# Second conv block read and multiplied ahead of the fifth modulation block, in a one-core diffusion layer on Trainium2

## The chip, the cores and the metric

The kernel runs on one core of one Trainium2 chip. The metric is the device time of one execution in microseconds (us). All times below are in us unless marked ns. PE is the matmul engine, PEld its weight load, DVE the vector engine, ACT the scalar engine, POOL the GpSimd engine, SP the engine whose queue issues nearly all loads.

## The reference

A layer with parallel token mixers and a mixture of experts, for 128 context tokens (s = 0) and 128 latent tokens (s = 1), 1024 channels, batch 1. The part around the change is the adaLN modulation and the combined input projection:

```python
mod = silu(c) @ w_ada + b_ada                 # 1024 x 6144; c_ctx for the context tokens
shift1, scale1, gate1, shift2, scale2, gate2 = split(mod, 6)
h = rmsnorm(x, norm1_g) * (1 + scale1) + shift1
z = h @ w_in                                  # 1024 x 8192
q, v, zf, zb, og, u, gz = split(z, ...)       # u: 2 x 512 columns of the conv branch
u = u[:, :512] * sigmoid(u[:, 512:])          # then a width-31 depthwise convolution
...                                           # gated linear recurrence with q, v, zf, zb
x1 = x + gate1 * (merged branches @ w_out)
x2 = x1 + gate2 * moe(rmsnorm(x1, norm2_g) * (1 + scale2) + shift2)
```

## The kernel before

Weights come in blocks of 1024 x 512 numbers (2048 KB each). `w_ada` has twelve of them and `w_in` sixteen. The list `blocks` fixes the order of the loads, and the sync engine's stream issues them in that order, one DMA each, from one line (L543). A block lies in one of four buffers, `ring[0]` to `ring[3]`, which the instruction listings below call ring_49 to ring_52. The table `place` says which. `load_block` waits until the block that had this buffer before is done with (`released`), and only then issues; everything behind it in the SP stream waits with it. Three rules of release matter here:

```python
if name in split[:apart]:
    eng.wait_ge(w_lo_done, 4 * split.index(name) + 4)
elif name[:3] == "ada":
    eng.wait_ge(part_ready, ADA.index(int(name[3:])) + 1)
elif name == "u1":
    eng.wait_ge(u1_part_ready, 1)
```

A modulation block (`ada...`) is used by `ada_partial(j)` (L1656 in `ada_partial`): eight matmuls of a padded 32-column condition vector with the block, 128x512 each, 16 in the records since each float32 matmul is recorded twice. The number j counts the blocks in the order 2, 3, 0, 1, 4, 5, ..., 11 (`ADA`), so j = 4 to 11 are the blocks ada4 to ada11. They accumulate in one bank, and the first of them, j = 4, opens it. Their sums (gates, second shift and scale) are first read behind the first quarter of block v0 (`ada_sums(2)`).

The projection blocks u2, q0, zf0, zb0, q1, zf1 and zb1 are multiplied in split precision: ACT rounds a quarter of the block to `w_hi` (L768), DVE computes the remainder `w_lo` (L1076), and PE runs three groups of eight matmuls per quarter, `h_hi` by `w_hi`, `h_hi` by `w_lo`, `h_lo` by `w_hi` (L1709, L1711, L1714 in `project_parts`). Such a block is released once DVE has split its last quarter. The modulated input is split too: `h_hi` on ACT (L783) and `h_lo` on DVE (L1100). ACT makes four of the eight channel blocks of `h_hi`, then the first quarter of `w_hi` of u2, then the other four, in this order of its program. The first conv block u1 is multiplied unsplit (L1695) with the modulation blocks j = 2 and 3 in the midst of it, followed by eight matmuls for its shift (L1787).

PE's program then runs ada_partial(4) and, for each of the seven names, its four quarters followed by one further modulation block, j = 5 to 11. Behind that come v0, v1 and the other projections (L1753, L1709 and so on), the recurrence (L1769, L1771), the merge and the experts (L2117, L2173), whose weights come in chunks of 1024 KB.

Of the kernel before, what the change touches and what calls it, by code (L numbers as in the profile page):

```python
# [132 lines left out]
def build(nc, A, outs):  # L133
    y_prompt, y_sample, new_state = outs
    ctx = ExitStack()
    with ctx:
# [186 lines left out]
        def cols(w, c0):  # L323
            return w.rearrange("(k p) c -> p k c", p=P)[:, :, c0:c0 + 512]
# [4 lines left out]

        ADA_GROUPS = ((0, 2), (2, 2), (4, 8))  # L330
        ada_group_of = [g for g, (_, n) in enumerate(ADA_GROUPS) for _ in range(n)]
        ada_sums_at = [256 + 8 * ADA[first] for first, _ in ADA_GROUPS]
        ada_after = {name: 4 + n for n, name in enumerate(("u1", "u2", "q0", "zf0", "zb0", "q1", "zf1", "zb1"))}
        col_of = {"u1": U0, "u2": U0 + 512, "v0": V0, "v1": V0 + 512}
        for half in range(2):
            for name, c0 in (("q", Q0), ("zf", ZF0), ("zb", ZB0), ("og", OG0), ("ga", GZ0), ("gb", GZ0 + 1024)):
                col_of[f"{name}{half}"] = c0 + 512 * half
        blocks = []
        for name in ("ada2", "ada3", "u1", "ada0", "ada1", "ada4", "u2", "q0", "ada5", "zf0", "ada6", "zb0", "ada7", "q1", "ada8", "zf1", "ada9", "zb1",
                     "ada10", "v0", "ada11", "v1", "og0", "og1", "ga0", "ga1", "gb0", "gb1"):  # L340
            blocks.append((name, cols(w_ada, 512 * int(name[3:])) if name[:3] == "ada" else cols(w_in, col_of[name])))
        blocks.append(("pc", A["w_proj_conv"][0].rearrange("(k p) c -> p k c", p=P)))
# [4 lines left out]
        apart = len(split)  # L347
        split += ["v0", "v1", "og0", "og1", "ga0", "ga1", "gb0", "gb1", "ph0", "ph1", "wo0", "wo1"]
        number = {name: n for n, (name, _) in enumerate(blocks)}


        place = {name: n % 4 for name, n in number.items()}
        for name, n in zip(("u2", "q0", "ada5", "zf0", "ada6", "zb0", "ada7", "q1", "ada8", "zf1", "ada9", "zb1", "ada10", "ada11"),
                           (3, 0, 2, 1, 3, 0, 2, 1, 3, 0, 2, 1, 3, 3)):
            place[name] = n
        for n, name in enumerate(("v0", "v1", "og0", "og1", "ga0", "ga1", "gb0", "gb1", "pc", "ph0", "ph1", "wo0")):
            place[name] = n % 3
# [22 lines left out]
        def tile_of(name):  # L380

            src = blocks[number[name]][1]
            k, n = src.shape[1], src.shape[2]
            return ring[place[name]][:, 0:k * n].rearrange("p (k c) -> p k c", k=k)
# [29 lines left out]
        for name, n, by in ([(f"xt{j}", 1, "act") for j in range(4)] + [(f"h{j}", 1, ("dve", "act")[j % 2]) for j in range(4)]  # L414
# [5 lines left out]
            for j in range(n):  # L420
# [3 lines left out]
                else:  # L424
                    n_dve += 1
                    fills.append((name, j, dve_evac, n_dve))
        fill_no = {(name, j): n for n, (name, j, _, _) in enumerate(fills)}

        def fill_bank(name, j=0):
# [107 lines left out]
        def _(sp):  # L537
            def load_block(name):

                before = in_place[place[name]].index(name) - 1  # L540
                if before >= 0:
                    released(sp, in_place[place[name]][before])
                sp.dma_start(tile_of(name), dict(blocks)[name]).then_inc(s_w[place[name]], 16)  # L543
# [5 lines left out]
                sp.dma_start(x_tok[:, s, :], x[0]).then_inc(s_x, 16)  # L549
            for name, _ in blocks[1:-2]:  # L550
                load_block(name)
                if name == "u2":
                    sp.dma_start(consts[:, C_MASK:C_TRI], A["consts"][:, C_MASK:C_TRI]).then_inc(s_wr, 16)
                    sp.dma_start(b_router[:, :], A["router_bias"].broadcast_to([P, NE])).then_inc(s_wr, 16)
            filled(sp, "gb1", 1)
# [72 lines left out]
            for step in range(FIXED_STEPS, NSTEPS):  # L628
# [10 lines left out]
                for part in range(3):  # L639
                    for item in range(ITEMS_OF[step]):  # L640
                        if part == 0:
                            j = FIRST_ITEM[step] + item
# [16 lines left out]
            n = sp.value_load(nwork, min_val=0, max_val=NX)  # L659
# [958 lines left out]
        def _(pe):  # L1618
            mm = nc.tensor.matmul

            def arrived(name):
                loaded(pe, name)
# [22 lines left out]
            def ada_partial(j):  # L1645

                g = ada_group_of[j]
                first, n = ADA_GROUPS[g]
                arrived(f"ada{ADA[j]}")
                if g == 2 and j == first:  # L1650
                    pe.wait_ge(part_copied, 1)
                w = tile_of(f"ada{ADA[j]}")
                window = slice(14 - 2 * (j - first), 46 - 2 * (j - first))
                for k in range(KD):
                    q = k % 4
                    ins = mm(bank[4 + g % 2][32 * q:32 * q + 32, :], c_pad[:, k, window], w[:, k, :], start=(j == first and k < 4), stop=(j == first + n - 1 and k >= 4))  # L1656
                ins.then_inc(part_ready, 1)
# [41 lines left out]
            def project_parts(name, q):  # L1699


                n = split.index(name)
                b = open_fill(name, q // 2) if q % 2 == 0 else fill_bank(name, q // 2)
                out = b[:, (q % 2) * T:(q % 2 + 1) * T]
                pe.wait_ge(w_lo_done, 4 * n + q + 1)
                for k in range(KD):
                    if (n, q) == (0, 0):
                        pe.wait_ge(h1_hi_done, k + 1)
                    mm(out, part_hi(n, q)[:, k, :], h1_hi[:, k, :], start=(k == 0), stop=False)  # L1709
                for k in range(KD):  # L1710
                    mm(out, part_lo(n, q)[:, k, :], h1_hi[:, k, :], start=False, stop=False)  # L1711
                pe.wait_ge(h1_lo_done, KD)
                for k in range(KD):
                    ins = mm(out, part_hi(n, q)[:, k, :], h1_lo[:, k, :], start=False, stop=(k == KD - 1))  # L1714
                ins.then_inc(proj_ready if q % 2 else w_used, 1)
# [70 lines left out]
                g = k % 4  # L1786
                ins = mm(bank[6][32 * g:32 * g + 32, :], shift_pad[:, k, :], tile_of("u1")[:, k, :], start=(k < 4), stop=(k >= 4))  # L1787
            ins.then_inc(u1_part_ready, 1)
            ada_partial(4)

            for name in ("u2", "q0", "zf0", "zb0", "q1", "zf1", "zb1"):

                for q in range(4):
                    project_parts(name, q)
                if name == "u2":
                    pe.wait_ge(u1_part_ready, 2)
                    for c in range(4):
                        ins = mm(bank[6][:, 2 * c:2 * c + 2], u1_part[:, c * P:(c + 1) * P], consts[:, C_SUM:C_SUM + NS], start=True, stop=True)
                    ins.then_inc(u1_bias_ready, 1)
                ada_partial(ada_after[name])  # L1800

            for level, name in zip(range(-1, LEVELS), ("v0", "v1", "og0", "og1", "ga0", "ga1", "gb0", "gb1")):
                quarter(name, 0)
# [529 lines left out]
```

## Time and profile before

| what | value |
| --- | --- |
| device time, median of 3 runs | 857.24 us (856.8 to 858.62) |
| the profiled execution: its own time | 856.77 us |
| the profiled execution: span | 854.9 us |
| PE busy | 801.4 us (94%) |
| PEld, DVE, ACT, POOL busy | 546.8, 384.8, 234.1, 20.9 us |
| DMA | 284.72 MB, 333 GB/s mean |
| chain that ended last, by engine | PE 68%, SP queue 17%, DMA 10%, DVE 3%, issue 2% |

The span is the time from the first to the last recorded instruction. The profiled execution's own time is 1.87 us longer than its span. The chain that ended last is followed back from the last instruction, at each step to what released it; a stretch of PE in it is a stretch in which any idle time of PE would lengthen the whole.

### The profile page before, as it was taken

The page shows a single profiled execution, that of the slowest core. Times are in us where ns is not written, and L with a number is a line of the kernel's source. Part 1 is how long each engine was busy: PE and PEld are TensorE (multiplying, and loading weights), DVE is VectorE, ACT ScalarE, POOL GpSimd, SP SyncE. Part 2 cuts the span into 40 slices and gives each one's busy share as a digit, 9 for nine tenths or more (in the row PEclk, how much of TensorE's full clock was granted, in tenths as well). Part 3 has the DMA queues.
Part 4 walks back from the last instruction along what each step waited for, and adds up shares of the span by engine and source line. Part 5 has one row for each costly group of instructions (what it writes and reads, how often), then busy time and mean ns, then how long its engine had stood idle before and what let it go on. Part 6 is the DMA issues. An engine that isn't in the chain of part 4 may idle for free.

```text
span 854.9 us, 12931 instructions
## 1 busy us (share of the span) xinstructions
PE 801.4 (94%) x5258; PEld 546.8 (64%) x5258; DVE 384.8 (45%) x789; ACT 234.1 (27%) x388; POOL 20.9 (2%) x22
## 2 busy tenths in 40 slices
PE   3989999999999989989999999599999999799974
PEld 1769898999999989955446355254554835355212
DVE  1157999879987566583323322112221112122114
ACT  2163747344354243231111111011121101011002
POOL 1000010100000000100000000000000000000000
PEclk9999999999999999999999999899999999899988
DMA  8998989323524649889999999999999999999995
GB/s 322 387 387 317 316 280 330 114 100 108 190 99 156 207 149 363 327 307 401 363 416 417 415 418 419 416 416 420 414 417 410 417 415 418 416 418 418 416 413 196
DMA packets 81222, 284.72 MB, mean 333 GB/s; under 512 B 5256, under 2 KB 12040, under 8 KB 64520
## 3 DMA queue, kind: packets, MB, share of 16 engines
q1 hardware_dynamic: 80664, 282.55, 85.0%
q10 hardware_dynamic: 496, 1.30, 0.4%
q8 instruction: 44, 0.72, 0.3%
q14 instruction: 18, 0.15, 0.0%
HBM read 280.67 MB, written 3.16 MB: 332 GB/s over the span
## 4 chain that ended last, share of the span: by engine, by line
PE 68%; SPq 17%; DMA 10%; DVE 3%; issue 2%; ACT 0%; POOL 0%; DVEq 0%; POOLq 0%
SPq L625 15%; PE bank L2117 12%; PE bank L2173 6%; PE bank L1709 6%; PE bank L1711 6%; PE bank L1714 6%; DMA chunk<-in_w_expert_gate_up 5%; PE bank L1695 3%; PE bank L2024 3%; PE bank L2001 3%; PE bank L1771 3%; PE bank L1753 3%; DMA chunk<-in_w_expert_down 3%; PE bank L1656 2%; PE bank L1731 2%
## 5 line engine op out<-in xcount | busy, mean ns | idle before, releaser
L2117 PE MATMUL bank<-chunk,xg 128*64 128x512 f32 (+2 forms) x1024 | 202.8, 627 | 19.0 <-DMA chunk<-in_w_expert_gate_up 18.8
L2117 PEld LDWEIGHTS bank<-chunk,xg 128*64 128x64 f32 (+2 forms) x1024 | 62.7, 131 | 152.4 <-issue 137.1
L2173 PE MATMUL bank<-chunk,act_t 128*64 128x512 f32 (+2 forms) x480 | 97.4, 613 | 1.8 <-DMA chunk<-in_w_expert_down 1.7
L1508 DVE SCALAR_TENSOR_TENSOR act_r<-bank,w_slot,sil 128x256 f32<-128x256 f32 x26 | 12.6, 484 | 182.2 <-ACT sil L981 182.2
L1520 DVE TENSOR_TENSOR y_lo<-bank,y_hi 128x512 fp32r<-128x512 f32 x52 | 35.9, 691 | 73.2 <-ACT y_hi L994 73.2
L981 ACT ACTIVATE sil<-bank 128x256 f32<-128x256 f32 x26 | 10.0, 384 | 210.9 <-PE bank L2117 210.9
L1076 DVE TENSOR_TENSOR ring_lo<-ring,ring_hi 128x1024 fp32r<-128x1024 f32 x44 | 52.7, 1219 | 19.9 <-ACT ring_hi L768 19.7
L2173 PEld LDWEIGHTS bank<-chunk,act_t 128*64 128x64 f32 (+2 forms) x480 | 30.0, 130 | 48.4 <-issue 47.5
L994 ACT ACTIVATE y_hi<-bank 128x512 fp32r<-128x512 f32 x52 | 30.9, 597 | 101.5 <-PE bank L2173 97.7
L1136 DVE SCALAR_TENSOR_TENSOR conv<-upad,dw,conv 128x256 f32<-128x256 f32 x120 | 52.8, 512 | 0.0
L768 ACT ACTIVATE ring_hi<-ring 128x1024 fp32r<-128x1024 f32 x44 | 44.4, 1052 | 25.6 <-PE bank L1735 14.1
L2001 PE MATMUL bank<-sel_p,h_hi 128*128 128x256 f32 x192 | 48.5, 294 | 0.0
L2001 PE MATMUL bank<-sel_p,h_lo 128*128 128x256 f32 x192 | 46.8, 282 | 0.0
L2024 PE MATMUL bank<-y_hi,sel_t 128*128 128x512 f32 x104 | 44.8, 431 | 1.4 <-DVE y_lo L1520 1.4
L1437 DVE COPY xg<-bank 128x512 f32<-128x512 f32 x26 | 17.9, 690 | 54.4 <-PE bank L2001 54.4
L2024 PE MATMUL bank<-y_lo,sel_t 128*128 128x512 f32 x104 | 40.9, 394 | 0.0
L1076 DVE TENSOR_TENSOR w_lo<-ring,w_hi 128x1024 fp32r<-128x1024 f32 x28 | 33.1, 1219 | 12.7 <-ACT w_hi L768 12.7
L2001 PEld LDWEIGHTS bank<-sel_p,h_hi 128*128 128x128 f32 x192 | 36.5, 190 | 0.5
L2001 PEld LDWEIGHTS bank<-sel_p,h_lo 128*128 128x128 f32 x192 | 36.6, 191 | 0.0
L2024 PEld LDWEIGHTS bank<-y_hi,sel_t 128*128 128x128 f32 x104 | 19.5, 187 | 24.3 <-issue 18.5
L1709 PE MATMUL bank<-h_hi,w_hi 128*128 128x256 f32 x224 | 32.4, 287 | 2.6 <-issue 2.6
L1709 PEld LDWEIGHTS bank<-h_hi,w_hi 128*128 128x128 f32 x224 | 28.8, 191 | 8.8 <-issue 6.0
(319 smaller groups left out, 1212.3 us busy)
## 6 DMA issues: line engine op xcount, KB each, us to landing
chunk<-in_w_expert_gate_up SPq DMA_DIRECT2D x128, 1024.0 KB, 21.1
chunk<-in_w_expert_down SPq DMA_DIRECT2D x63, 1024.0 KB, 22.5
ring<-in_w_in SPq DMA_DIRECT2D x16, 2048.0 KB, 10.2
ring<-in_w_ada SPq DMA_DIRECT2D x12, 2048.0 KB, 14.5
ring<-in_w_proj_hgrn SPq DMA_DIRECT2D x2, 2048.0 KB, 7.9
ring<-in_w_out SPq DMA_DIRECT2D x2, 2048.0 KB, 13.8
ring<-in_w_proj_conv SPq DMA_DIRECT2D x1, 2048.0 KB, 7.8
chunk<-in_w_shared_gate_up SPq DMA_DIRECT2D x2, 1024.0 KB, 22.9
```

The source lines that it names most:

```text
L625: sp.dma_start(dst, src).then_inc(s_chunk[place], 16)
L768: nc.scalar.activation(part_hi(n, q), tile_of(split[n])[:, :, q * P:(q + 1) * P], ACT.Copy).then_inc(w_hi_done, 1)
L1076: V.tensor_tensor(part_lo(n, q), tile_of(split[n])[:, :, q * P:(q + 1) * P], part_hi(n, q).bitcast(F32), ALU.subtract).then_inc(w_lo_done, 1)
L1136: ins = V.scalar_tensor_tensor(dst, src, tap, dst, ALU.mult, ALU.add)
L1520: V.tensor_tensor(y_lo[h][:, :], bank[(3 - b, 2 + b)[h]][:, :], y_hi[h][:, :].bitcast(F32), ALU.subtract).then_inc(y_ready, 1)
L1709: mm(out, part_hi(n, q)[:, k, :], h1_hi[:, k, :], start=(k == 0), stop=False)
L1711: mm(out, part_lo(n, q)[:, k, :], h1_hi[:, k, :], start=False, stop=False)
L1714: ins = mm(out, part_hi(n, q)[:, k, :], h1_lo[:, k, :], start=False, stop=(k == KD - 1))
L2001: ins = mm(bank[part % 2][:, c * 2 * P:(c + 1) * 2 * P], src[:, s, k, :], sel_p[:, s, :], start=(n == 0), stop=(n == 3))
L2024: ins = mm(y_acc[s][h][:, :], sel_t[b][:, s * P:(s + 1) * P], part[h][:, :], start=(first and part is y_hi), stop=(last and part is y_lo))
L2117: ins = mm(bank[2 + b][row:row + width, :], xg[:, k, c:c + width], w[:, k % 4, :], start=(k == 0), stop=(k == KD - 1))
L2173: ins = mm(out[row:row + width, :], act_t[:, c, row:row + width], w[:, c, h * 512:(h + 1) * 512], start=(c == 0), stop=(c == 1))
```

## The change

It alters three tables and one position in PE's program. In `blocks`, u2 moves ahead of ada4. In `place`, u2 goes to `ring[1]` and ada4 to `ring[3]`, the reverse of before. In PE's program, ada_partial(4) leaves its position ahead of u2, and each of the seven names is now followed by the modulation block that used to be one position earlier: u2 by j = 4, q0 by 5, zf0 by 6, zb0 by 7, q1 by 8, zf1 by 9, and zb1 by two, 10 and 11.

```diff
-        ada_after = {name: 4 + n for n, name in enumerate(("u1", "u2", "q0", "zf0", "zb0", "q1", "zf1", "zb1"))}
+        ada_after = {name: (4 + n,) for n, name in enumerate(("u2", "q0", "zf0", "zb0", "q1", "zf1"))}
+        ada_after["zb1"] = (10, 11)
...
-        for name in ("ada2", "ada3", "u1", "ada0", "ada1", "ada4", "u2", "q0", "ada5", "zf0", "ada6", "zb0", "ada7", "q1", "ada8", "zf1", "ada9", "zb1",
+        for name in ("ada2", "ada3", "u1", "ada0", "ada1", "u2", "ada4", "q0", "ada5", "zf0", "ada6", "zb0", "ada7", "q1", "ada8", "zf1", "ada9", "zb1",
                      "ada10", "v0", "ada11", "v1", "og0", "og1", "ga0", "ga1", "gb0", "gb1"):
...
-        for name, n in zip(("u2", "q0", "ada5", "zf0", "ada6", "zb0", "ada7", "q1", "ada8", "zf1", "ada9", "zb1", "ada10", "ada11"),
-                           (3, 0, 2, 1, 3, 0, 2, 1, 3, 0, 2, 1, 3, 3)):
+        for name, n in zip(("u2", "ada4", "q0", "ada5", "zf0", "ada6", "zb0", "ada7", "q1", "ada8", "zf1", "ada9", "zb1", "ada10", "ada11"),
+                           (1, 3, 0, 2, 1, 3, 0, 2, 1, 3, 0, 2, 1, 3, 3)):
...
-                if name == "u2":
+                if name == "ada4":
...
-            ada_partial(4)
...
-                ada_partial(ada_after[name])
+                for j in ada_after[name]:
+                    ada_partial(j)
```

The numbers behind zb1, ada10 and ada11 in the last table are 1, 3, 3 before and after: ada10 and ada11 use the same buffer, `ring[3]`. The two small loads in the SP stream (masks and router bias) stand behind the same position of the stream as before, the load into `ring[3]` ahead of q0's.

PE's program behind the unsplit block u1, before. The row with ring_50 and `c_pad` is ada_partial(4):

```order
L1695 MATMUL bank<-x_gained,ring_51 128x256 x4
L1787 MATMUL bank<-ring_51,shift_pad 32x512 x8
L1656 MATMUL bank<-ring_50,c_pad 32x512 x8
L1709 MATMUL bank<-h_hi,w_hi 128x256 x8
L1711 MATMUL bank<-h_hi,w_lo 128x256 x8
L1714 MATMUL bank<-h_lo,w_hi 128x256 x8
```

The same place in the changed kernel (its lines are numbered one higher):

```order
L1696 MATMUL bank<-x_gained,ring_51 128x256 x4
L1788 MATMUL bank<-ring_51,shift_pad 32x512 x8
L1710 MATMUL bank<-h_hi,w_hi 128x256 x8
L1712 MATMUL bank<-h_hi,w_lo 128x256 x8
L1715 MATMUL bank<-h_lo,w_hi 128x256 x8
```

The modulation block is gone from between the shift of u1 and the first quarter of u2.

PE's program at the end of zb1 and the start of v0 (L1753), before. The row with `c_pad` is ada_partial(11); ada_partial(10) stands ahead of the twelve rows of zb1's four quarters, of which the last is shown:

```order
L1714 MATMUL bank<-h_lo,w_hi 128x256 x8
L1656 MATMUL bank<-ring_52,c_pad 32x512 x8
L1753 MATMUL bank<-w_hi,h_hi 128x256 x8
L1753 MATMUL bank<-ring_lo_79,h_hi 128x256 x8
L1753 MATMUL bank<-w_hi,h_lo 128x256 x8
```

The same place in the changed kernel:

```order
L1715 MATMUL bank<-h_lo,w_hi 128x256 x8
L1657 MATMUL bank<-ring_52,c_pad 32x512 x16
L1754 MATMUL bank<-w_hi,h_hi 128x256 x8
L1754 MATMUL bank<-ring_lo_79,h_hi 128x256 x8
L1754 MATMUL bank<-w_hi,h_lo 128x256 x8
```

Both of the last two modulation blocks, 8 matmuls each and both read from ring_52, now stand next to each other.

The loads in the SP stream from zb1 on (zb1, ada10, v0, ada11, v1, og0), with what each waits for; these rows are the same before and after but for the line number, here of the changed kernel. In both, the load of ada11 waits until ada_partial(10) is done:

```order
L544 DMA ring_50<-in_w_in 128x8x512 [waits w_lo_done]
L544 DMA ring_52<-in_w_ada 128x8x512 [waits ada_partial]
L544 DMA ring_49<-in_w_in 128x8x512 [waits w_lo_done]
L544 DMA ring_52<-in_w_ada 128x8x512 [waits ada_partial]
L544 DMA ring_50<-in_w_in 128x8x512 [waits w_lo_done]
L544 DMA ring_51<-in_w_in 128x8x512 [waits ada_partial]
```

No row moved here. What moved is the point in PE's program at which the awaited partial ends.

## Rows read from the trace of the kernel before

**Rows 1.** The chain that ended last, in order of time: start, duration, what.

```profile
45.53 1.72 PE bank L1656 x16
47.25 2.58 issue
...
130.54 1.85 PE bank L1656 x16
...
144.09 1.85 PE bank L1656 x16
...
146.56 3.10 PE bank L1753 x24
```

**Rows 2.** Stretch from v0 to 290: busy time of each engine, clock, DMA share, GB/s.

```profile
146.56:290.00 143.44, 143.44 (x1139) 141.33 (x1140) 123.23 (x150) 59.13 (x74) 5.36 (x2) 1.00 0.40 136
```

**Rows 3.** PE's waits in all from 145 on: total, times, longest.

```profile
PE bank L2117 <- DMA chunk<-in_w_expert_gate_up: 18.8, 7, 6.3
PE bank L2173 <- DMA chunk<-in_w_expert_down: 1.7, 1, 1.7
```

**Rows 4.** Timeline around u2's start: start, duration, engine, line, tiles, [idle before <-releaser].

```profile
42.16 2.45 ACT L783 ACTIVATE h_hi<-x_gained,mod 128x128 fp32r<-128x128 f32 x8 [2.36 <-DVE mod L1062]
...
47.41 1.06 ACT L768 ACTIVATE w_hi<-ring 128x1024 fp32r<-128x1024 f32 x1 [2.80 <-DMA ring<-in_w_in]
...
49.82 1.42 PE L1709 MATMUL bank<-h_hi,w_hi 128*128 128x256 f32 x8 [2.58 <-issue]
...
53.75 2.36 DVE L1076 TENSOR_TENSOR w_lo<-ring,w_hi 128x1024 fp32r<-128x1024 f32 x2 [0.73 <-ACT w_hi L768]
...
71.08 2.00 ACT L768 ACTIVATE w_hi<-ring 128x1024 fp32r<-128x1024 f32 x2
```

**Rows 5.** Timeline of the SP queue: issues of ring blocks.

```profile
10.00 16.26 SPq L543 DMA_DIRECT2D ring<-in_w_ada  x3
...
81.35 0.37 SPq L543 DMA_DIRECT2D ring<-in_w_in  x1
81.76 0.58 SPq L543 DMA_DIRECT2D ring<-in_w_ada  x1
...
132.46 0.37 SPq L543 DMA_DIRECT2D ring<-in_w_ada  x1
136.30 59.10 SPq L543 DMA_DIRECT2D ring<-in_w_in  x5
```

**Rows 6.** DMA issues around 20.9: queue, count, size, us to landing.

```profile
ring<-in_w_ada SPq DMA_DIRECT2D x1, 2048.0 KB, 21.0
```

**Rows 7.** The same view around 81.35 and 81.76.

```profile
ring<-in_w_in SPq DMA_DIRECT2D x1, 2048.0 KB, 10.6
ring<-in_w_ada SPq DMA_DIRECT2D x1, 2048.0 KB, 15.4
```

**Rows 8.** The same view around 132.46.

```profile
ring<-in_w_ada SPq DMA_DIRECT2D x1, 2048.0 KB, 8.2
```

**Rows 9.** PE's timeline at restarts: the kernel's start and the expert stage.

```profile
11.02 3.49 PE L1656 MATMUL bank<-ring,c_pad 128*32 128x512 f32 x16 [3.49 <-DMA ring<-in_w_ada]
...
19.03 1.92 PE L1656 MATMUL bank<-ring,c_pad 128*32 128x512 f32 x16 [2.61 <-DMA ring<-in_w_ada]
...
535.82 3.64 PE L2117 MATMUL bank<-chunk,xg 128*32 128x512 f32 x32 [1.11 <-DMA chunk<-in_w_expert_gate_up]
...
545.77 5.78 PE L2117 MATMUL bank<-chunk,xg 128*32 128x512 f32 x32 [6.30 <-DMA chunk<-in_w_expert_gate_up]
```

**Rows 10.** Stretches around the wait that ends at 545.77, columns as in rows 2.

```profile
543.00:544.00 1.00, 0.00 (x0) 0.00 (x0) 0.00 (x0) 0.00 (x0) 0.00 (x0) 0.65 0.96 397
...
549.00:550.00 1.00, 1.00 (x8) 0.22 (x4) 0.00 (x0) 0.00 (x0) 0.00 (x0) 0.50 0.98 393
550.00:551.00 1.00, 1.00 (x16) 0.34 (x8) 0.00 (x0) 0.00 (x0) 0.00 (x0) 0.94 1.06 422
```

**Rows 11.** The SP queue's own waits and its timeline ahead of the expert chunks.

```profile
SPq L569 <- ACT s_new L896: 20.1, 1, 20.1
...
312.44 2.40 SPq L566 DMA_DIRECT2D chunk<-in_w_expert_gate_up  x3
```

**Rows 12.** Stretch from 315 to 360, columns as in rows 2.

```profile
315.00:360.00 45.00, 44.95 (x381) 44.42 (x380) 29.01 (x52) 16.61 (x22) 3.77 (x2) 1.00 0.99 374
```

## The prediction

> **What bounds the kernel now.** I read the chain of waits first, since the change lies in one stage of a kernel whose PE is busy nearly throughout. Up to the end of the input projections it is almost all PE. The one idle piece near the edit is 2.58 us at 47.25, behind the fifth modulation block and ahead of u2 [rows 1]. The timeline says what it waited for: ACT had made half of `h_hi` from 42.16 to 44.61, then sat 2.80 us until u2 landed, and only at 47.41 rounded its first quarter; PE started at 49.82 [rows 4]. So the early bound is the landing of u2. From 49.82 to the start of v0 at 146.56 PE runs block after block, with 0.61 us idle at the end (144.09 + 1.85 = 145.94 to 146.56) [rows 1]. From 146.56 to 290 PE is busy in 143.44 of 143.44 us [rows 2]: any time added ahead of v0 comes out at 290 in full.
>
> **What the change does at the start.** In the changed kernel u2 takes the transfer that ada4 had. That one was the last of the three issues of 10.00 to 26.26, sent as soon as the second modulation block was used, around 20.9, and it landed 21.0 us later, at 41.9 [rows 5, 6]. That is before `h_hi` begins. ACT therefore rounds the first quarter of u2 straight behind the first half of `h_hi`, at about 44.5 instead of 47.41. Everything that follows on ACT, DVE and PE is chained to it, so PE starts u2 at 49.82 - 2.9 = 46.9. This is not 2.9 us of gain, for the modulation block's 1.85 us [rows 1] has only been put off: PE's idle time shrinks from 2.58 to 46.9 - 45.5 = 1.4 us, a gain of 1.2. Bounds: nothing (if u2 is still late) to 1.2.
>
> **In the middle.** The seven projections and the partials between them keep their number and order, each partial is simply one index lower, so PE reaches each point 2.9 us earlier. Each modulation block j now leaves its buffer one block later, so each reload is issued one step later: 144.09 - 130.54 = 13.55 less the 2.9, 10.65 us. For ada5 to ada10 the block is also wanted one step later. For ada10: the partial j = 8 is over at 144.09 - 2.9 - 2 x 13.55 + 1.85 = 115.9, a second load of a close pair took 15.4 us [rows 7], so ada10 is there at 131.4, and is wanted at 141.2. One projection load has a new release: zf0 takes `ring[1]` once DVE has split u2, at 53.75 + 2.36 - 2.9 = 53.2, and ACT first wants it at 71.08 - 2.9 = 68.2 [rows 4]. That is 15.0 us for a load that needs 10.6 to 15.4 [rows 7]. I take nothing, at most 0.4.
>
> **At the end of the row of blocks.** Here the step is not hidden. ada10 and ada11 share `ring[3]`. Before, PE used ada10 at 130.54, ahead of zb1; SP issued ada11 at 132.46 [rows 1, 5], 0.07 us after the end at 132.39; it landed 8.2 us later, at 140.7 [rows 8]; PE wanted it at 144.09. The cover was zb1's four quarters, and 3.4 us of it was left. Now both partials stand behind zb1 with nothing between them. PE uses ada10 from 141.2 to 143.0 and then needs a block whose load may only be issued at 143.1. PE is in order and waits.
>
> The wait ends when 2048 KB have landed. Two prices stand in the trace. Alone in the queue, ada11 took 8.2 us [rows 8]. With another block issued 0.41 us behind it, q1 at 81.35 took 10.6 [rows 5, 7], and the pair was in after 81.76 + 15.4 - 81.35 = 15.8 us. The new place is like the second: behind ada11 the SP stream holds v1 and og0, whose buffers are long free (v1 went out at 136.30 [rows 5]), so both follow within a microsecond. I take 10.6; the bounds are 8.2 and, for a third load in the same queue, 10.6 + (10.6 - 8.2) = 13.0. The Trainium skill ("DMA: Bandwidth & Descriptors", section "Queues, rings and completion order") says that on each DMA engine descriptors are consumed in ring order. By that, loads behind ada11 would not hold it up, and the sum would take 8.2.
>
> Then the restart. PE will have been idle some 10.8 us. The longest wait in the expert stage was 6.30 us: the granted clock fell to 0.50 during it (mean 0.65 in 543 to 544) and was back only around 550, and the 32 records behind the wait took 5.78 us against 3.64 for 32 behind a wait of 1.11 [rows 9, 10]. That is 1.2 GHz for 2.4 and 2.1 us lost. The kernel's start shows a smaller price for the very instruction at hand: 3.49 us for the first modulation block, 1.92 for the second, 1.6 lost [rows 9]. I take 2.1, since the idle time is of the longer sort, with 1.6 and 3.0 as bounds (3.0 if v0's first quarter, 3.10 us long [rows 1], runs half of its time slowly as well as ada11: 1.6 + 1.4).
>
> **The sum.** ada10 ends 143.0; issue + 0.1; landing + 10.6 = 153.7; pick-up + 0.1; ada11's matmuls 1.85; low clock 2.1: v0 starts at 157.8. Its halves of `w_lo` are then long split, so the 0.61 us of waiting is gone (already in this sum). Against 146.56 that is 11.2 us later. By its parts: - 1.2 at the start, + 10.8 of waiting, + 2.1 of clock, - 0.6 of waiting saved.
>
> Who waits behind it: SP's stream. v1 and og0 go out at 143.5 instead of 136.30, and v1 lands at about 159. ACT, which splits v1 next, has until v0's first column half is done, some 10 us after v0 starts, before PE wants the next block. So this is covered. Afterwards nothing gives the time back. PE has no idle time until 290. The expert chunks start at 312.44, behind a 20.1 us wait of SP for ACT's copy of the final states [rows 11], which is itself behind PE, and from there the DMA engines run at 0.99 of their time [rows 12], so they start as much later as PE does and end as much later.
>
> The rows are of the profiled execution, which took 856.77 us by its own time, 0.47 below the median shown. 856.77 + 11.2 = **868.0**. With the lower bounds (8.2 and 1.6) it is 11.2 - 2.4 - 0.5 = 8.3 later, 865.1; with the upper (13.0, 3.0) 14.5 later, 871.3.
>
> **Rivals.**
> 1. *Queue order.* ada11 goes first through every DMA engine and lands in 8.2 us. Everything else as forecast: + 8.8, 865.6. For it: ada11 is issued 0.4 us ahead of v1. Against it: q1 was ahead of its partner by as much and took 10.6.
> 2. *No earlier start of u2.* If something else than its landing holds the first quarter (DVE's share of `h_lo`, say), the early 2.9 us are lost. PE then reaches v0 2.9 us later than forecast: 870.9. Against it: ACT's 2.80 us of waiting for exactly this load [rows 4].
> 3. *Given back in the expert stage.* PE waits 18.8 + 1.7 = 20.5 us there for chunks [rows 3]. If the chunks kept their times while PE came 11.2 us late, these waits would swallow the delay and the time would be about 857, no change. It decides at the first chunk's issue: this needs it to stay at 312.44, and [rows 11] ties it to PE's work.
> 4. *The change pays.* If ada11 were hidden as before, only the gain of 1.2 at the start and up to 0.6 ahead of v0 would be left: 855.0 to 855.6, faster. It needs ada11's load to be issued by about 134 (8.2 to 10.6 us ahead of 143.0), and ring[3] is then still held by ada10.
>
> **How the numbers follow.** The forecast as it stands 0.60, queue order 0.20, no earlier start 0.08, anything larger still 0.05, given back 0.04, pays 0.03. A difference of 0.2% (1.7 us) is about what a measurement of this kernel can tell from none. Faster is rival 4, 0.03; within 0.2% is most of rival 3, 0.03; slower is the rest, 0.94. The range runs from 864.0, a little below the sum with lower bounds for the 0.47 and for drift in the expert stage, to 871.5, the sum with upper bounds, and takes in rivals 1 and 2.
>
> **What would show it.** In the profile of the changed kernel: u2's first matmul at about 46.9; each of the seven blocks 2.9 earlier; a wait of PE for the DMA of w_ada of 8 to 13 us at 143, the longest in the kernel; a granted clock of 0.50 at its end and the matmuls of ada11 near 3.5 us; v0 near 157.8; the expert stage starting some 11 us later with PE's total wait for chunks close to 20.5. The prediction is wrong if that wait of PE is short or missing, or if the waits for chunks shrink by as much as it adds.

## The result: 7.8 us slower, and the profile after

The changed kernel takes 865.38 us (median of 6 runs, 864.62 to 865.81), the kernel before 857.6 in the same measurement (856.8 to 858.66). The ratio is 1.0089, with a 95% interval of 1.0078 to 1.0100: slower, where 868.0 was forecast.

The page of the profile after, its span and PE's line, and the head of its chain that ended last:

```profile
span 862.7 us, 12931 instructions
...
PE 800.8 (93%) x5258; PEld 546.2 (63%) x5258; DVE 384.9 (45%) x789; ACT 234.3 (27%) x388; POOL 20.9 (2%) x22
...
PE 66%; SPq 18%; DMA 10%; DVE 3%; issue 2%; ACT 0%; POOL 0%; DVEq 0%; POOLq 0%
```

The span is 7.8 us longer than the 854.9 of before, and PE is not busier: the time is waiting. The chain that ended last says where (start, duration, what; answers to [rows 1]):

```profile
45.66 1.38 issue
...
127.76 1.85 PE bank L1657 x16
...
141.32 1.90 PE bank L1657 x16
143.24 8.00 DMA ring<-in_w_ada
151.28 3.31 PE bank L1657 x16
154.59 3.06 PE bank L1754 x24
```

The idle time ahead of u2 fell from 2.58 to 1.38 us. ada10 is used at 141.32, and then the chain leaves PE for the load of ada11, 8.00 us long. ada11's own matmuls take 3.31 us where ada10's took 1.90, and v0 starts at 154.6 instead of 146.56, 8.0 us later. The rest of the kernel keeps that: 862.7 - 154.6 = 708.1 us from there to the end, against 854.9 - 146.56 = 708.3.

The timeline after around the start of u2 (answers to [rows 4]):

```profile
42.29 2.45 ACT L784 ACTIVATE h_hi<-x_gained,mod 128x128 fp32r<-128x128 f32 x8 [2.36 <-DVE mod L1063]
...
44.64 1.04 ACT L769 ACTIVATE w_hi<-ring 128x1024 fp32r<-128x1024 f32 x1
...
47.04 1.42 PE L1710 MATMUL bank<-h_hi,w_hi 128*128 128x256 f32 x8 [1.38 <-issue]
```

ACT no longer waits between the two. The SP queue's timeline after (answers to [rows 5]):

```profile
121.01 0.37 SPq L544 DMA_DIRECT2D ring<-in_w_in  x1
143.24 0.37 SPq L544 DMA_DIRECT2D ring<-in_w_ada  x1
143.65 91.83 SPq L544 DMA_DIRECT2D ring<-in_w_in  x7
```

SP issues nothing from 121.01 to 143.24: it stands at ada11, which waits for ada10's matmuls, and v1 and og0 stand behind it. The view of DMA issues, around 143.24 to 143.7 (count, size, us to landing; answers to [rows 8]):

```profile
ring<-in_w_ada SPq DMA_DIRECT2D x1, 2048.0 KB, 8.0
ring<-in_w_in SPq DMA_DIRECT2D x1, 2048.0 KB, 13.0
```

ada11 lands in 8.0 us although v1 and og0 follow it at once; v1, issued 0.41 us later, is in 5.4 us after ada11. The stretches after around the wait (PE, PEld, DVE, ACT, POOL busy, granted clock, DMA share, GB/s; answers to [rows 10]):

```profile
147.00:148.00 1.00, 0.00 (x0) 0.00 (x0) 1.00 (x2) 0.00 (x0) 1.00 (x1) 0.65 1.06 412
...
153.00:154.00 1.00, 1.00 (x12) 0.19 (x4) 0.00 (x0) 0.00 (x0) 0.00 (x0) 0.50 1.04 383
154.00:155.00 1.00, 1.00 (x12) 0.48 (x5) 0.00 (x0) 0.27 (x1) 0.00 (x0) 0.93 1.05 385
```

The granted clock is down to 0.50 (1.2 GHz) before PE resumes at 151.28 and full again (2.4 GHz) soon after 154: ada11's matmuls run at the low level up to their last 0.4 us or so, and v0 loses nothing. The waits of PE after 60 (total, times, longest; answers to [rows 3]):

```profile
PE bank L2118 <- DMA chunk<-in_w_expert_gate_up: 19.7, 7, 6.3
PE bank L1657 <- DMA ring<-in_w_ada: 8.1, 1, 8.1
PE bank L2174 <- DMA chunk<-in_w_expert_down: 2.4, 1, 2.4
```

The waits for expert chunks have not shrunk. The delay was not given back there.

### The profile page after: what moved, and what is told of

Same layout as the page of the kernel before. It is cut to its first block, busy times and chain, and to the rows that moved or that the text cites. A ratio compares the mean times of both kernels' runs of the same rounds, so it can differ in the third digit from the quotient of the medians.

```text
span 862.7 us, 12931 instructions
## 1 busy us (share of the span) xinstructions
PE 800.8 (93%) x5258; PEld 546.2 (63%) x5258; DVE 384.9 (45%) x789; ACT 234.3 (27%) x388; POOL 20.9 (2%) x22
## 4 chain that ended last, share of the span: by engine, by line
PE 66%; SPq 18%; DMA 10%; DVE 3%; issue 2%; ACT 0%; POOL 0%; DVEq 0%; POOLq 0%
SPq L626 16%; PE bank L2118 11%; PE bank L2174 6%; PE bank L1710 6%; PE bank L1712 6%; PE bank L1715 6%; DMA chunk<-in_w_expert_down 5%; PE bank L1696 3%; PE bank L2002 3%; PE bank L1772 3%; PE bank L2025 3%; PE bank L1754 3%; DMA ring<-in_w_ada 3%; PE bank L1657 3%; DMA chunk<-in_w_expert_gate_up 2%
## 5 line engine op out<-in xcount | busy, mean ns | idle before, releaser
L2118 PE MATMUL bank<-chunk,xg 128*64 128x512 f32 (+2 forms) x1024 | 200.9, 618 | 19.9 <-DMA chunk<-in_w_expert_gate_up 19.7
L1657 PE MATMUL bank<-ring,c_pad 128*32 128x512 f32 x192 | 25.9, 663 | 14.5 <-DMA ring<-in_w_ada 14.5
L1077 DVE TENSOR_TENSOR w_lo<-ring,w_hi 128x1024 fp32r<-128x1024 f32 x28 | 33.1, 1222 | 10.6 <-ACT w_hi L769 10.6
```

Of the source, the lines that this page charges most:

```text
L1077: V.tensor_tensor(part_lo(n, q), tile_of(split[n])[:, :, q * P:(q + 1) * P], part_hi(n, q).bitcast(F32), ALU.subtract).then_inc(w_lo_done, 1)
L2118: ins = mm(bank[2 + b][row:row + width, :], xg[:, k, c:c + width], w[:, k % 4, :], start=(k == 0), stop=(k == KD - 1))
```

## The experiments

The theory under test: the whole loss is one load, ada11's, which can't be issued before ada10's matmuls have read the buffer that both use; it costs its own latency plus a slow restart of PE. Unless said otherwise the edits are to the changed kernel.

### ada11 in a buffer of its own

```diff
-                           (1, 3, 0, 2, 1, 3, 0, 2, 1, 3, 0, 2, 1, 3, 3)):
+                           (1, 3, 0, 2, 1, 3, 0, 2, 1, 3, 0, 2, 1, 3, 2)):
```

Expected: 

> The changed kernel with ada11 in the buffer that ada9 leaves, instead of in ada10's. Theory A (the whole loss is the load of ada11 that can't be issued before ada10 is used): the wait of 8.1 us and the slow restart of 1.4 go, v0 starts at about 145.0 to 145.2 where it started at 154.6 in the changed kernel and at 146.6 before, and the time is 1.3 to 1.8 below the kernel before, about 856. Theory B (the delay comes from the two partials behind zb1 or from the later loads as such, and ada11's wait only stands where another would): v0 still starts at 150 or later and the time stays above 860.

Measured: 855.38 us (8 runs) against 857.63 for the kernel before, ratio 0.9972 (0.9962 to 0.9983). The chain of this kernel:

```profile
141.44 3.57 PE bank L1657 x32
145.01 3.07 PE bank L1754 x24
```

Both modulation blocks run as one piece, nothing waits, and v0 starts at 145.01. One number in a table takes away the whole loss and leaves the early gain. This run shows that the two partials behind zb1 cost nothing as such.

### ada10 used behind zf1

```diff
-        ada_after["zb1"] = (10, 11)
+        ada_after["zf1"] = (9, 10)
+        ada_after["zb1"] = (11,)
```

Expected: 

> The changed kernel with ada10 used behind zf1, next to ada9, and ada11 alone behind zb1; the buffers are as in the changed kernel. Theory A: ada11 may be issued at about 131.5, lands by 140, and is hidden behind zb1 again, so v0 starts at 145.1 and the time equals that of the kernel with the buffer exchanged, about 856. Theory B: the pair of partials costs what it cost behind zb1, now at 129, and the time stays above 860.

Measured: 856.02 us (12 runs) against 857.63, ratio 0.9983 (0.9975 to 0.9992). PE's timeline in this kernel:

```profile
142.86 1.92 PE L1658 MATMUL bank<-ring,c_pad 128*32 128x512 f32 x16
144.71 1.22 PE L1755 MATMUL bank<-w_hi,h_hi 128*128 128x256 f32 x8
```

The buffer is shared again, but the four quarters of zb1 stand between the two uses, and the wait is gone. What matters is the work between the two uses of one buffer.

### PE's new order with the old loads

```diff
-        for name in ("ada2", "ada3", "u1", "ada0", "ada1", "u2", "ada4", "q0",
+        for name in ("ada2", "ada3", "u1", "ada0", "ada1", "ada4", "u2", "q0",
...
-                           (1, 3, 0,
+                           (3, 0,
```

The list of names in that second table loses ada4 with its number, and the two small loads stand where the kernel before has them.

Expected: 

> PE's new order with the loads and buffers of before: u2 lands at 47.4 as before, ada4 at 42. Theory A: u2's first matmul is at 49.8 to 49.9, all blocks are 2.8 later than in the changed kernel, and the wait at the end is the same 8 us plus the slow restart, so v0 starts at about 157.4 and the time is about 10.8 above before, 868.3. Theory B, in which the early start of u2 buys nothing: the time equals the changed kernel's, 865.4.

Measured: 869.75 us (4 runs) against 857.63, ratio 1.0139 (1.0122 to 1.0156), 1.4 above the expectation. PE's timeline and, behind it, one stretch of this kernel:

```profile
50.34 1.61 PE L1710 MATMUL bank<-h_hi,w_hi 128*128 128x256 f32 x8 [4.43 <-issue]
...
156.16 3.64 PE L1657 MATMUL bank<-ring,c_pad 128*32 128x512 f32 x16 [8.19 <-DMA ring<-in_w_ada]
```

```profile
51.00:52.00 1.00, 1.00 (x7) 0.84 (x6) 1.00 (x6) 1.00 (x3) 0.00 (x0) 0.60 1.06 387
```

The early start of u2 counts in full: without it everything is later, and v0 starts at 159.7, 5.2 us behind the changed kernel. Of that, 3.3 us are u2's start (50.34 against 47.04). The rest is what I had left out: with nothing to multiply ahead of u2, PE idles 4.43 us, and behind that the granted clock falls (mean 0.60 in 51 to 52), so that from u2's start to the end of its sums some 1.3 us more go by than in the changed kernel. At the end of the row PE waits as long as in the changed kernel (8.19 us against 8.11), but the restart costs 0.6 more: ada11's matmuls take 3.64 us against 3.31, and v0's first group 1.52 against 1.21.

### ada11 last in the queue

```diff
-                     "ada10", "v0", "ada11", "v1", "og0", "og1",
+                     "ada10", "v0", "v1", "og0", "ada11", "og1",
```

Expected: 

> The changed kernel with the loads of v1 and og0 issued ahead of ada11's, which then has nothing behind it in the queue until v0 has been used. Theory A, with the price of the prediction (a block right behind lengthens a load, 10.6 against 8.2): can't hold as 8.0 was measured with two blocks behind; if it held at all ada11 would land quicker than 8.0 here. Rival (queue order: what stands behind costs nothing): ada11 lands 7.7 to 8.2 us after its issue, v0 starts at 154.6 and the time is that of the changed kernel, 865.4, within 0.5.

Measured: 868.96 us (4 runs) against 857.63, ratio 1.0131 (1.0112 to 1.0150), 3.6 above the changed kernel. Neither reading had foreseen this. The chain of this kernel, behind it v0's first group in PE's timeline and the stretch in which ada11 is issued:

```profile
143.34 11.41 DMA ring<-in_w_ada
154.75 0.04 issue
154.79 3.64 PE bank L1657 x16
```

```profile
158.36 2.08 PE L1754 MATMUL bank<-w_hi,h_hi 128*128 128x256 f32 x8
```

```profile
143.00:144.00 1.00, 0.27 (x4) 0.00 (x0) 1.00 (x2) 1.00 (x2) 0.00 (x0) 1.00 0.99 285
```

The load took 11.4 us. v1 and og0 went out from 133.6 on, and at 143 the DMA engines were still busy at 0.99 of their time with og0. It landed 15.5 us after its issue at 134.0, at 149.5, and ada11 5.2 us behind it, much as v1 landed 5.4 us behind ada11 in the changed kernel. So ada11 had to let og0 pass, and what stands ahead in the queue lengthens a load. What stands behind doesn't: 8.0 us in the changed kernel with two blocks behind. Why og0 itself landed 7.6 us behind v1 and not 5.4 is open, and about 2 of the 3.4 us that ada11's load grew by are due to that.

The restart is dearer here too: ada11's matmuls take 3.64 us and v0's first group 2.08 against 1.21, together some 2.6 us lost. The granted clock is back only soon after 160, 5.6 us after PE resumed.

### PE kept busy through the wait

```diff
                 for j in ada_after[name]:
+                    if j == 11:
+                        pe.wait_ge(s_wr, 32)
+                        for _ in range(17):
+                            mm(bank[6][:, 0:512], ident, consts[:, C_MASK:C_MASK + 512], start=True, stop=True)
                     ada_partial(j)
```

Expected: 

> The changed kernel with 17 matmuls added in front of ada11's, on data long in place and into a bank that nobody reads, about 7.6 us of PE work inside the wait of 8.1. They wait for nothing that is late, so the load of ada11 is issued and lands as before. Theory (1.4 us of the loss are a low clock after the wait, since PE was idle): ada11's matmuls take 1.9 instead of 3.3, the granted clock stays 1.00 through the stage, v0 starts at 153.2 instead of 154.6, and the time is about 864.0 against 865.4. Rival (the first matmuls behind a late load are slow for another reason, e.g. the load's last bytes): they stay at 3.3 and the time at 865.4.

Measured: 870.47 us (5 runs) against 858.15, ratio 1.0149 (1.0135 to 1.0163). The fill was twice as long as meant, and so this run says nothing by its time. PE's timeline:

```profile
143.28 14.86 PE L1804 MATMUL bank<-consts 128*128 128x512 f32 x34
158.07 1.93 PE L1657 MATMUL bank<-ring,c_pad 128*32 128x512 f32 x16
```

Each added matmul took 0.87 us in two records. The second row answers the question all the same: ada11's matmuls take 1.93 us when PE comes to them busy, and the granted clock is 1.00 throughout. The next kernel has eight of them:

Expected: 

> As the kernel with 17 added matmuls, with 8 of them, since one took 0.87 us and 17 took 14.8. 8 take 7.0 us and end at about 150.4, before ada11's load lands at 151.4. Theory (the low clock after the wait is part of the loss): PE then waits only 1 us for the load, ada11's matmuls take 1.9, v0 starts at 153.3 to 153.5 against 154.6 in the changed kernel, and the time is 1.1 to 1.4 below the changed kernel's 865.4, about 864.1. Rival: ada11's matmuls take 3.3 as in the changed kernel and the time stays at 865.4.

Measured: 863.1 us (5 runs) against 858.16, ratio 1.0062 (1.0048 to 1.0076). PE's timeline:

```profile
143.31 7.13 PE L1804 MATMUL bank<-consts 128*128 128x512 f32 x16
151.54 1.92 PE L1657 MATMUL bank<-ring,c_pad 128*32 128x512 f32 x16 [1.10 <-DMA ring<-in_w_ada]
153.40 1.22 PE L1754 MATMUL bank<-w_hi,h_hi 128*128 128x256 f32 x8
```

PE waits only 1.10 us, ada11's matmuls take 1.92 against 3.31, and v0 starts at 153.4 instead of 154.5 (ada10 was 0.2 later in this execution, so 1.1 of the 1.4 show). The slow restart is part of the loss. Added work made the changed kernel faster: the interval of its ratio to the kernel before lies, if barely, below the changed kernel's 1.0078 to 1.0100. The time is 2.3 us below the changed kernel's, twice what v0 gained; the two were measured apart, and I put no cause on the rest.

### ada10 in the midst of zb1

```diff
-        ada_after["zb1"] = (10, 11)
+        ada_after["zb1"] = (11,)
...
                 for q in range(4):
                     project_parts(name, q)
+                    if (name, q) == ("zb1", 1):
+                        ada_partial(10)
```

Expected: 

> The changed kernel with ada10's matmuls in the midst of zb1, behind its second quarter, so that 5.8 us of matmuls stand between ada10 and ada11. Theory A (a load of 8.1 us, covered by what PE has to do between the two): ada11 is issued at about 137.4 and lands at 145.4, PE waits 2.2 us instead of 8.1, too short for the clock to fall, v0 starts at 147.4 and the time is 0.8 above before, about 858.4. A rival in which the position behind zb1 itself costs: less than half of the 7.8 us goes.

Measured: 860.29 us (5 runs) against 858.15, ratio 1.0028 (1.0015 to 1.0042). More than half of the loss is gone, as theory A has it, but 1.9 us less than it said. PE's timeline, and behind it the stretches of the restart:

```profile
147.04 2.55 PE L1657 MATMUL bank<-ring,c_pad 128*32 128x512 f32 x16 [3.21 <-DMA ring<-in_w_ada]
149.52 2.08 PE L1754 MATMUL bank<-w_hi,h_hi 128*128 128x256 f32 x8
```

```profile
147.00:148.00 1.00, 0.96 (x12) 0.36 (x16) 1.00 (x2) 1.00 (x3) 0.00 (x0) 1.00 1.06 391
148.00:149.00 1.00, 1.00 (x12) 0.06 (x4) 1.00 (x3) 0.62 (x2) 0.30 (x1) 0.60 1.06 389
149.00:150.00 1.00, 1.00 (x6) 0.48 (x3) 1.00 (x2) 0.30 (x1) 1.00 (x1) 0.50 1.06 389
```

The wait was 3.21 us, 1.0 longer than reckoned, as the load took 9.0 (of the sixteen completion records that the trace has of it, fifteen stand within 8.0 us and the last alone at 9.0). And the clock did fall, but only after PE had resumed, between 148 and 149: part of ada11 (2.55 us against 1.9) and the first group of v0 (2.08 against 1.2) were slow, together some 1.6 us.

With the same edit behind the first quarter (`("zb1", 0)`), 8.8 us of matmuls stand between the two:

Expected: 

> The changed kernel with ada10's matmuls behind the first quarter of zb1, so that 8.8 us of matmuls stand between it and ada11. Theory A: ada11 is issued at about 134.5 and lands 8.0 to 9.0 later, PE waits 0 to 0.5 us for it, no slow restart, v0 starts at 145.1 to 145.7, the time is that of the kernel with the buffer exchanged, 855.4 to 856.0. Rival (any wait, however short, brings the slow restart as the wait of 3.2 us did): v0 starts at 146.5 or later, 857.0 or more.

Measured: 855.85 us (9 runs) against 858.16, ratio 0.9981 (0.9972 to 0.9991). PE's timeline:

```profile
143.46 1.93 PE L1657 MATMUL bank<-ring,c_pad 128*32 128x512 f32 x16
145.32 1.22 PE L1754 MATMUL bank<-w_hi,h_hi 128*128 128x256 f32 x8
```

No wait and no slow restart. With 0, 5.8, 8.8 and 11.7 us of matmuls between the two uses of `ring[3]` (changed kernel, midway, first quarter, behind zf1), v0 starts at 154.5, 149.5, 145.3 and 144.7: the loss is the part of one load that is not covered, and the slow restart where the clock falls (changed kernel and midway).

### The new loads alone

To the kernel before, only the new order of the two loads and their buffers; PE still multiplies ada4 ahead of u2.

```diff
-        for name in ("ada2", "ada3", "u1", "ada0", "ada1", "ada4", "u2", "q0",
+        for name in ("ada2", "ada3", "u1", "ada0", "ada1", "u2", "ada4", "q0",
...
-                           (3, 0,
+                           (1, 3, 0,
```

The list of names in that second table gains ada4 with its number.

Expected: 

> The new order of the two loads and their buffers with PE's order of before. ada4 now lands at 47.5 and is multiplied first, so PE waits about 1.9 us for it at 45.6 and goes on to u2 at 49.3, whose first quarter is ready since 46.9. Theory A: 0.4 to 0.5 us of idle time are saved at the start, ada11 is hidden as before, and at v0 nothing more is saved than this; the time is 0 to 0.5 below before, no difference that can be told. Rival (the new load order is what slows the kernel): slower by several us.

Measured: 855.38 us (8 runs) against 858.15, ratio 0.9974 (0.9963 to 0.9984). That is 2.8 us below, more than expected. PE's timeline:

```profile
47.18 1.93 PE L1656 MATMUL bank<-ring,c_pad 128*32 128x512 f32 x16 [1.50 <-DMA ring<-in_w_ada]
...
49.03 1.21 PE L1709 MATMUL bank<-h_hi,w_hi 128*128 128x256 f32 x8
...
145.40 1.19 PE L1753 MATMUL bank<-w_hi,h_hi 128*128 128x256 f32 x8 [0.61 <-issue]
```

v0 starts 1.16 us earlier than before (146.56). I had counted 0.5: u2 started 0.8 earlier, since ada4 landed at 47.1 and not 47.5, and the 0.3 us that u2's first quarter lost to ACT's last pieces of `h_hi` went too (1.21 us for its first group against 1.42 [rows 4]). The profiled span is 1.6 us shorter than before's, the median 2.8. Much of that difference is in the execution of before that was profiled: it took 856.77, and the median of its runs is 857.6 to 858.2, while this kernel's profiled execution, at 855.11, was near its median. From trace to trace the gain is 1.7, of which 1.2 stand at v0.

### The new loads and the buffer of its own together

The kernel just shown, with ada10 and ada11 both behind zb1 and nothing behind zf1, and ada11 in `ring[2]`.

Expected: 

> The new load order with PE's order of before at the start (ada4 ahead of u2) and the pair ada10, ada11 behind zb1, ada11 in ada9's old buffer. Sum of the two gains found: PE idles 1.5 us ahead of ada4 and nowhere before v0, the 0.61 us in front of v0 are gone, v0 starts at 144.8. Time 855.0 to 855.4, no difference from the two kernels of which it is made (855.4 each) that can be told. If it is slower, one of the two gains depends on the other place being as it was.

Measured: 855.73 us (7 runs) against 858.16, ratio 0.9972 (0.9961 to 0.9983). No difference from the two that it is made of. v0 did not start at 144.8. The timeline, DVE and PE:

```profile
143.53 2.34 DVE L1078 TENSOR_TENSOR ring_lo<-ring,w_hi 128x1024 fp32r<-128x1024 f32 x2
...
145.97 1.19 PE L1755 MATMUL bank<-w_hi,h_hi 128*128 128x256 f32 x8 [0.93 <-issue]
```

PE got there earlier and waited 0.93 us instead, until 0.1 us after DVE had split the first half of v0 (143.53 + 2.34 = 145.87). DVE comes to that split only behind twenty steps of the convolution, 8.00 us without a pause. Here DVE sets v0's start, so moving the last partials of PE can't bring it forward. DVE's work hangs on u2, which starts at 49.6 here and at 49.0 with the new loads alone, since ada4 landed 0.6 us later in this execution; that is the 0.57 us by which v0 starts later than the 145.40 of that kernel.

## Why the prediction was right, and where its sizes were off

**What bounds it, and the early gain.** As predicted. u2's first matmul is at 47.04 (46.9 forecast), the idle time 1.38 us (1.4 forecast), and PE ran 2.8 us ahead of before from there to the partial behind zb1 (141.32 against 144.09). That the earlier landing of u2 is worth this, is shown by PE's order with the old loads. The rival in which u2 starts no earlier is out.

**The middle.** As predicted: PE waits for no load between u2 and ada11.

**The wait at the end.** The mechanism is shown three ways: by the chain of the changed kernel, by its going away with a buffer of its own, and by its shrinking with the matmuls put between. The step whose size was off is "I take 10.6". The load took 8.0, and the reason that I gave for 10.6, that v1 and og0 go out right behind, is wrong. I had weighed the Trainium skill's rule ("DMA: Bandwidth & Descriptors", "Queues, rings and completion order": on each DMA engine descriptors are consumed in ring order) against the one pair of loads at 81.35 and believed the pair. The traces agree with the rule: 8.0 us with two blocks behind, 11.4 with one still in flight ahead. What made q1 take 10.6 at 81.35 [rows 7] is open; it was not a block ahead, and in the last-in-queue kernel v1 took 8.3 with a block as close behind. The trace's sixteen completion records show that only parts of q1 were late: they stand from 7.1 to 10.6 us after its issue, where those of ada11 in the changed kernel stand from 7.4 to 8.0.

**The restart.** "I take 2.1" measured 1.4: ada11's 3.31 us against 1.90. The clock was back about 2.9 us after PE resumed (151.28 to soon after 154), where it had taken 4.3 in the expert stage (545.77 to soon after 550, [rows 9, 10]), so that v0 lost nothing. 2.1 was no bad price all the same: with PE's new order and the old loads a wait of the same length cost 2.0, and the clock took 4.3 us to come back. When it comes back is not shown to follow from the length of the wait. The lower price of 1.6, taken from the kernel's start [rows 9], was misread. The granted clock was full there, as in this stretch of the kernel before (columns as in [rows 2]):

```profile
12.00:13.00 1.00, 1.00 (x12) 0.30 (x8) 0.00 (x0) 0.00 (x0) 0.00 (x0) 1.00 0.99 389
```

So what made the first modulation block take 3.49 us is open, and that row prices no low clock.

**The sum.** By its parts: - 1.2 at the start, + 8.1 of waiting (10.8 forecast), + 1.4 of clock (2.1), - 0.6 ahead of v0, in sum + 7.7; v0 is 8.0 later. Of the rest, 0.1 is this execution's own drift (its second modulation block began at 19.16 against 19.03), and 0.1 to 0.2 is that the moved block, 1.72 us in the chain at its old place [rows 1], takes 1.85 to 1.9 at a new one. Time in the end: + 7.8. The 3.3 us between 157.8 and 154.5 are 2.7 of the wait and 0.7 of the clock, less rounding. So the forecast of 868.0 had the mechanism right and its delay of 11.2 us too long by 3.4, and the range held because it also took in the price without blocks behind. What happened is the rival of queue order, to which I had given 0.20. That its 865.6 stands beside the measured 865.38 is in part luck: its delay of 8.8 us is 1.0 too long (the clock at 2.1), and it was added to 856.77, the time of one quick execution, where the kernel before has a median of 857.6.

**Nothing given back.** From v0's start to the end of the span every kernel here took 707.9 to 709.5 us, with v0 at 144.7 (behind zf1) to 159.9 (17 added matmuls). That rules out the rival in which the expert stage swallows the delay: PE's waits for gate and up chunks there were 18.6 to 19.7 us in all of them, whatever happened before.

**Did the change pay?** As it stands it doesn't. With one number altered it does, by 2.3 us (0.9972). But the new loads alone, with PE's order left as it was, take the same 855.38 us (0.9974): the gain comes from the earlier landing of u2, and no run shows that moving the partials in PE's program adds to it.

## What to carry to other kernels

When a use of a buffer is moved, look at the next load into that buffer: it can be issued only once that use is over, and the work left between this use and the next must cover a whole load (here 8 to 9 us for 2048 KB). A shift of all uses by one place keeps that distance everywhere except at the end of the row, where two uses meet; that is the place to reckon. And price an exposed wait of the matmul engine with its restart, and as a range: here 1.3 us on top of a wait of 4.4, 1.6 on one of 3.2, 1.4 and 2.0 on waits of 8.1 and 8.2, and 2.6 on one of 11.5.

## What the runs showed of the hardware

- The clock can fall after PE has resumed. Behind a wait of 3.21 us it was 1.00 while PE was idle and fell between 148 and 149, 1 to 2 us into the work; behind the wait of 4.43 us (PE's new order with the old loads) it fell between 51 and 52, with PE at work since 50.34. Waits of 1.1 us (eight added matmuls) and 2.58 us (before, ahead of u2) brought no slow matmuls; 3.21, 4.43, 8.1 and 11.5 did.
- The same wait does not bring the same restart. Behind 8.11 us the clock was back 2.9 us after PE resumed, behind 8.19 us 4.3.
- Filling a wait with useless matmuls is worth time. Eight of them took 1.1 us off v0's start.
- A matmul of a 128x128 weight block with 512 float32 columns took 0.87 us (14.86 us for 17). Eight with 32 weight columns each took 1.92 together, 0.24 apiece, so the first row can't be priced from the second.
- A 2048 KB load took 8.0 to 9.0 us at this place with nothing ahead of it, whether blocks followed it or not, and 11.4 with the rest of one block ahead.
